# Block inverses in the recurrence: transposes on VectorE, predicated copies for masked subtractions, and a new order on ScalarE

## The chip, the cores and the metric

The kernel runs on one core of one Trainium2 chip, in one launch. The metric is the time of one execution on the device, in microseconds (us); several executions are run and the median is taken.

## The reference, cut to what matters

Two layers of a decoder trunk over 512 tokens of width 1024. Layer 0 mixes the tokens with two linear recurrences of 8 heads x 64 each, an RWKV-7 group and a gated DeltaNet group. Both need, for each chunk of 64 tokens and each head, the inverse of a unit lower triangular 64x64 matrix (below in the form of the second group; the first is a scan over tokens that the kernel also computes by chunks):

```python
a_mat = jnp.where(strict, jnp.einsum('bhnik,bhnjk->bhnij', k_beta, k) * decay, 0.0) + jnp.eye(C, dtype=f32)
tri = functools.partial(lax.linalg.triangular_solve, left_side=True, lower=True, unit_diagonal=True)
u = tri(a_mat, v * beta[..., None])
w = tri(a_mat, k_beta * jnp.exp(g)[..., None])
...
def step(S, inp):
    v_new = u_c - jnp.einsum('bhck,bhkv->bhcv', w_c, S)
    o_c = jnp.einsum('bhck,bhkv->bhcv', q_c * jnp.exp(g_c)[..., None], S) + jnp.einsum('bhij,bhjv->bhiv', qk_c, v_new)
    S = S * jnp.exp(g_last)[..., None] + jnp.einsum('bhck,bhcv->bhkv', k_c * jnp.exp(g_last - g_c)[..., None], v_new)
```

Around it stand large projections and MLPs, and in layer 1 two attention groups; the change doesn't touch them.

## The kernel before

The program has one instruction list per engine, written out by hand, and semaphores between them. Layer 0's input projection comes first, then the recurrence, then layer 0's output projection and MLP, then layer 1.

**The recurrence** is a loop over s = 0 to 4. For s < 4 it prepares block s of 128 tokens (two chunks of 64, one on partitions 0 to 63, the other on 64 to 127, for 8 heads side by side in 512 columns): it is "ahead". For s > 0 it runs the states of block m = s - 1 through its two chunks and makes that block's output: it is "behind". The two kinds of work are interleaved in each engine's list, and each engine keeps its order. So s = 0 has only the preparation, s = 1 to 3 have both, and s = 4 has only the work behind.

**The inverse.** R stands for the RWKV heads, G for the gated heads. `QI` holds the transposed inverse so far (it begins as the 2x2 blocks, masked by VectorE, with the identity added by GpSimd), `TI` the inverse itself, `LT` the full triangle. `first_inverse` transposes `QI` into `TI`. Then come five levels, in which blocks of 2, 4, 8, 16 and 32 rows are joined to blocks of twice the size. A level in `level_products` is: TensorE multiplies `LT` by `TI` for R and then G (banks 0 and 1); VectorE multiplies by the mask `MERGE[:, lev + 1]` into `XM` (L1644); TensorE multiplies `QI` by `XM`; VectorE subtracts the result from `TI` (L1647). `level_turn` has TensorE transpose `TI` for R and G, with matmuls against the identity into banks 2 and 3 (L664), and ScalarE copies them to `QI` (L1181), which only the second product of the next level reads. The last level takes the factors the other way round and changes `QI` directly, so that no transposition follows it.

**What stands between the levels.** Each product or transposition by `both_halves` (L602) or `transposed` (L664) is 16 matmul calls of 64x64, and each fp32 call shows as two instructions. TensorE puts the work behind between the levels: `state_sums` and `chunk_out` (L719, L602) after level 0, `turned_out` (L579), the transposition of the output rows, before level 4. VectorE puts `chunk_out` (L1682 to L1688) and the next block's `decay_steps` (L1598) between levels 1 and 2, `out_var` (L1692 to L1697) after level 2, `out_scaled` (L1701, L1702) and the next block's `scaled_rows` (L1603, L1604) between levels 3 and 4. ScalarE runs `out_squares` (L1185, L1187) after the turn of level 1, `out_rms` (L1191, L1193, each with a table load) and the next block's `decays` (L1135, L1137) after that of level 2, before that of level 3. GpSimd scales two tensors of the next block (L2008, L2009) as soon as the first of the `decays` is there. The next block's inputs (L629, L579) wait for the last level's result (`inv_done`).

## Time and profile before

| | |
|---|---|
| median of 3 runs | 1593.75 us (1593.73 to 1594.44) |
| the profiled execution | 1590.02 us |
| its span, from the first to the last instruction | 1588.2 us |
| TensorE busy in it | 1480.8 us (93%) |
| VectorE, ScalarE, GpSimd busy | 724.6 us (46%), 601.9 us (38%), 574.5 us (36%) |
| mean granted TensorE clock | 0.97 of full |
| the recurrence | from about 250 to 491 us of the span |

PE is TensorE, DVE VectorE, ACT ScalarE, POOL GpSimd. A busy share is a mean over stages with different limits; for the change the stretch of the recurrence is what has to be read. The profiled execution is one execution, not one of the three of the median.

### The profile page before, as it was taken

The page shows a single profiled execution, that of the slowest core. Times are in us where ns is not written, and L with a number is a line of the kernel's source. Part 1 is how long each engine was busy: PE and PEld are TensorE (multiplying, and loading weights), DVE is VectorE, ACT ScalarE, POOL GpSimd, SP SyncE. Part 2 cuts the span into 40 slices and gives each one's busy share as a digit, 9 for nine tenths or more (in the row PEclk, how much of TensorE's full clock was granted, in tenths as well). Part 3 has the DMA queues.
Part 4 walks back from the last instruction along what each step waited for, and adds up shares of the span by engine and source line. Part 5 has one row for each costly group of instructions (what it writes and reads, how often), then busy time and mean ns, then how long its engine had stood idle before and what let it go on. Part 6 is the DMA issues. An engine that isn't in the chain of part 4 may idle for free.

```text
span 1588.2 us, 27117 instructions
## 1 busy us (share of the span) xinstructions
PE 1480.8 (93%) x11601; PEld 1193.2 (75%) x11601; DVE 724.6 (46%) x1065; ACT 601.9 (38%) x866; POOL 574.5 (36%) x266
## 2 busy tenths in 40 slices
PE   5999888989987999999999799996989999999998
PEld 4787568888885788888888588773457888888886
DVE  4787775686655341313222602885843413223131
ACT  4424453243334431313232424547854413233231
POOL 4343331010002344343434323233954343443432
PEclk9999899999978999999999899997999999999999
DMA  4332100000011322323223312220002332323231
GB/s 127 89 93 80 53 27 3 4 3 4 4 55 60 100 90 96 105 81 105 87 98 97 89 54 87 73 80 0 1 28 80 106 97 89 106 79 106 79 106 53
DMA packets 128403, 110.18 MB, mean 69 GB/s; under 512 B 10678, under 2 KB 126512, under 8 KB 128304
## 3 DMA queue, kind: packets, MB, share of 16 engines
q1 hardware_dynamic: 126944, 107.06, 21.6%
q8 instruction: 80, 1.31, 0.4%
q10 hardware_dynamic: 1360, 1.65, 0.3%
q14 instruction: 19, 0.16, 0.0%
HBM read 106.60 MB, written 2.10 MB: 68 GB/s over the span
## 4 chain that ended last, share of the span: by engine, by line
PE 76%; DVE 12%; ACT 7%; issue 3%; POOL 1%; ACTq 1%; DVEq 0%; POOLq 0%
PE ps L476 20%; PE ps L481 20%; PE ps L477 20%; PE ps L602 5%; PE ps L664 2%; DVE lower L1864 2%; DVE lower L1860 1%; POOL lower L2066 1%; DVE upper L1467 1%; PE ps L617 1%; PE ps L610 1%; ACT lower L1368 1%; PE ps L579 1%; PE ps L719 1%; PE ps L822 0%
## 5 line engine op out<-in xcount | busy, mean ns | idle before, releaser
L2034 POOL TENSOR_TENSOR w_lo<-lower,w_hi 128x2048 fp32r<-128x2048 f32 x84 | 387.6, 4614 | 642.0 <-ACT w_hi L1024 642.0
L476 PE MATMUL ps<-h_hi,w_hi 128*128 128x512 f32 x792 | 316.0, 399 | 8.9 <-ACT h_hi L1029 5.9
L477 PE MATMUL ps<-h_hi,w_lo 128*128 128x512 f32 x792 | 314.7, 397 | 0.0
L1024 ACT ACTIVATE w_hi<-lower 128x2048 fp32r<-128x2048 f32 x84 | 160.2, 1907 | 242.8 <-PE ps L481 242.8
L481 PE MATMUL ps<-h_lo,w_hi 128*128 128x512 f32 x792 | 201.6, 395 | 0.4
L476 PE MATMUL ps<-a_hi,w_hi 128*128 128x512 f32 x480 | 189.1, 394 | 0.0
L477 PE MATMUL ps<-a_hi,w_lo 128*128 128x512 f32 x480 | 189.1, 394 | 0.0
L476 PEld LDWEIGHTS ps<-h_hi,w_hi 128*128 128x128 f32 x792 | 150.3, 190 | 46.4 <-issue 11.5
L477 PEld LDWEIGHTS ps<-h_hi,w_lo 128*128 128x128 f32 x792 | 150.4, 190 | 36.1 <-issue 0.5
L481 PEld LDWEIGHTS ps<-h_lo,w_hi 128*128 128x128 f32 x792 | 148.7, 188 | 37.4 <-DVE h_lo L1574 1.7
L1809 DVE TENSOR_TENSOR lower<-lower,ps 128x512 f32<-128x512 f32 x64 | 44.0, 688 | 268.7 <-PE ps L481 268.7
L1793 DVE SCALAR_TENSOR_TENSOR lower<-ps,lower 128x512 f32<-128x512 f32 x64 | 44.3, 692 | 226.0 <-PE ps L481 209.9
L2013 POOL TENSOR_TENSOR pw_lo<-lower,pw_hi 128x1024 fp32r<-128x1024 f32 (+1 forms) x31 | 79.0, 2550 | 127.0 <-ACT pw_hi L1036 127.0
L1255 ACT ACTIVATE lower<-lower 128x512 f32<-128x512 f32 x64 | 40.5, 633 | 215.9 <-DVE lower L1793 215.9
L481 PE MATMUL ps<-a_lo,w_hi 128*128 128x512 f32 x480 | 121.5, 395 | 0.0
L476 PE MATMUL ps<-x_hi,pw_hi 128*128 128x512 f32 (+1 forms) x248 | 101.4, 409 | 5.7 <-issue 4.3
L481 PEld LDWEIGHTS ps<-a_lo,w_hi 128*128 128x128 f32 x480 | 90.1, 188 | 21.7
L477 PEld LDWEIGHTS ps<-a_hi,w_lo 128*128 128x128 f32 x480 | 90.1, 188 | 21.4
L476 PEld LDWEIGHTS ps<-a_hi,w_hi 128*128 128x128 f32 x480 | 90.0, 188 | 21.1
L1798 DVE TENSOR_TENSOR h_lo<-lower,h_hi 128x512 fp32r<-128x512 f32 x64 | 97.3, 1521 | 6.9 <-ACT h_hi L1257 6.9
L477 PE MATMUL ps<-x_hi,pw_lo 128*128 128x512 f32 (+1 forms) x248 | 99.2, 400 | 0.0
L602 PE MATMUL ps<-lower 64*64 64x64 f32 x2112 | 69.7, 219 | 6.4 <-DVE upper L1632 3.0
(352 smaller groups left out, 2092.7 us busy)
## 6 DMA issues: line engine op xcount, KB each, us to landing
lower<-in_mlp_w_dram SPq DMA_DIRECT2D x64, 1024.0 KB, 5.2
lower<-in_ev_w_in_dram SPq DMA_DIRECT2D x30, 512.0 KB, 3.8
lower<-in_od_w_in_dram SPq DMA_DIRECT2D x10, 1024.0 KB, 5.2
lower<-in_ev_w_out_dram SPq DMA_DIRECT2D x4, 1024.0 KB, 5.2
lower<-in_od_w_out_dram SPq DMA_DIRECT2D x4, 1024.0 KB, 5.0
out_dram<-lower SPq DMA_DIRECT2D x4, 512.0 KB, 3.2
lower<-in_od_w_in_dram SPq DMA_DIRECT2D x6, 256.0 KB, 3.8
upper<-in_x_dram ACTq DMA_DIRECT2D x1, 1024.0 KB, 8.4
```

Of the source, the lines that this page charges most:

```text
L476: pe.matmul(o, wh, xh, start=(i_ == 0), stop=False)
L477: pe.matmul(o, wl, xh, start=False, stop=False)
L481: mm = pe.matmul(o, wh, xl, start=False, stop=(i_ == n_ - 1))
L602: mm = pe.matmul(ps[part, b, h_ * HD:(h_ + 1) * HD], mats[part, j, q, :], vals[part, j, q, :], start=(start and h_ == 0), stop=True, skip_ ...
L664: mm = pe.matmul(ps[part, b, h_ * HD:(h_ + 1) * HD], x[part, h_ // 2, h_ % 2, :], IDENT[part, part], start=True, stop=True)
L1024: act.activation(WH[:, u % 2, :, 0:w], RAW[:, u % 2, :, 0:w], ACT.Copy).then_inc(hi_ready, 1)
L1255: act.activation(sq, sq, ACT.Square).then_inc(h1_sq, 1)
L1793: dve.scalar_tensor_tensor(out=SQT[:, b % 4, :], in0=src(q)[:, :], scalar=0.0, in1=RS[2 * l + 1], op0=ALU.max, op1=mul).then_inc(bank_read, 1)
L1798: dve.tensor_tensor(HL[:, b, :], SQT[:, b % 4, :], as_f32(HH[:, b, :]), sub).then_inc(h1_ready, 1)
L1809: dve.tensor_tensor(XT[:, k, :], XT[:, k, :], src(q_m2[l] + k)[:, :], add)\
L2013: pool.tensor_tensor(PWL[:, u % 3, :, 0:w], PRAW[:, u % 2, :, 0:w], as_f32(PWH[:, u % 3, :, 0:w]), ALU.subtract).then_inc(pw_lo, 1)
L2034: pool.tensor_tensor(WL[:, u % 2, :, 0:w], RAW[:, u % 2, :, 0:w], as_f32(WH[:, u % 2, :, 0:w]), ALU.subtract)\
```

## The change

1. **Transposes.** TensorE's `first_inverse` and `level_turn` go, with ScalarE's and VectorE's copies behind them. VectorE transposes in 32x32 blocks from SBUF to SBUF: `QI` to `TI` at the start, `TI` to `QI` after levels 0 to 3. Up to then no block of the inverse is larger than 32x32, so that a blockwise transposition is the whole one.
2. **Joining.** The first product of a level is not masked: ScalarE copies it from PSUM with the factor -1. VectorE then writes the second product into `TI` (or, in the last level, `QI`) only where the mask is set, with `copy_predicated`. The last level's mask is built for the upper side.
3. **Order.** `level_products` is split into `below_blocks` and `joined_blocks`. ScalarE's copies of level 2 stand ahead of `out_squares`, those of level 3 ahead of `out_rms`, those of level 4 behind `out_rms` and `decays`. On TensorE the first products of level 4 stand ahead of `turned_out`, the second ones behind it. Two semaphores go, and with them TensorE's wait for `inv_q` at the start of a block.

```diff
@@ TensorE
             def turned_inputs(s):
                 pe.wait_ge(e_gtri, s + 1)
                 if s > 0:
-                    pe.wait_ge(inv_q, 2 * (LAST - 1) * s)
                     pe.wait_ge(inv_done, 2 * s)
...
-            def transposed(b, x, done):
-            def first_inverse(s):
-            def level_turn(s, lev):
-            def level_products(s, lev):
+            def below_blocks(s, lev):
                 n = 2 * LAST * s + 2 * lev
                 for g, (lt, ti) in enumerate(((LTR, TIR), (LTG, TIG))):
-                    pe.wait_ge(inv_t, n + g + 1)
+                    pe.wait_ge(inv_t, n + (2 if lev == 0 else g + 1))
                     both_halves(g, lt, ti, True).then_inc(inv_x, 1)
+
+            def joined_blocks(s, lev):
+                n = 2 * LAST * s + 2 * lev
                 for g, (qi, xm) in enumerate(((QIR, XMR), (QIG, XMG))):
                     pe.wait_ge(inv_xm, n + g + 1)
...
                 if ahead:
-                    level_turn(s, 0)
                     for lev in range(1, LAST - 1):
-                        level_products(s, lev)
-                        level_turn(s, lev)
+                        below_blocks(s, lev)
+                        joined_blocks(s, lev)
+                    below_blocks(s, LAST - 1)
                 if behind:
                     turned_out(m)
                 if ahead:
-                    level_products(s, LAST - 1)
+                    joined_blocks(s, LAST - 1)
@@ ScalarE
-            def first_inverse(s):
-            def level_turn(s, lev):
-                for g, qi in enumerate((QIR, QIG)):
-                    act.wait_ge(inv_turn, 2 * (LAST - 1) * s + 2 * lev + g + 1)
-                    act.activation(flat4(qi[s % 2]), bank[2 + g], ACT.Copy).then_inc(inv_q, 1)
+            def below_blocks(s, lev):
+                for g, xm in enumerate((XMR, XMG)):
+                    act.wait_ge(inv_x, 2 * LAST * s + 2 * lev + g + 1)
+                    act.activation(flat4(xm), bank[g], ACT.Copy, scale=-1.0).then_inc(inv_xm, 1)
...
                 if ahead:
-                    level_turn(s, 0)
-                    level_turn(s, 1)
+                    below_blocks(s, 0)
+                    below_blocks(s, 1)
                 else:
                     weight_hi(0)
+                if ahead:
+                    below_blocks(s, 2)
                 if behind:
                     out_squares(m)
                 if ahead:
-                    level_turn(s, 2)
+                    below_blocks(s, 3)
                 if behind:
                     out_rms(m)
                 if s < TT - 1:
                     decays(s + 1)
                 if ahead:
-                    level_turn(s, 3)
+                    below_blocks(s, 4)
@@ VectorE
+            def blocks(m):
+                return m.bitcast(I32).unsqueeze(1).unsqueeze(1).broadcast_to([P, PAIRS, 2, HD])
...
             def first_inverse(s):
-                dve.wait_ge(inv_t0, 2 * s + 1)
-                dve.wait_ge(inv_t, 2 * LAST * s + 1)
-                dve.tensor_copy(TIG, by_head(bank[1])).then_inc(inv_t, 1)
-
-            def level_products(s, lev):
+                for g, (ti, qi) in enumerate(((TIG, QIG), (TIR, QIR))):
+                    dve.wait_ge(inv_q0, 2 * s + g + 1)
+                    dve.transpose(flat4(ti), flat4(qi[s % 2])).then_inc(inv_t, 1)
+
+            def joined_blocks(s, lev):
                 n = 2 * LAST * s + 2 * lev
-                for g, xm in enumerate((XMR, XMG)):
-                    dve.wait_ge(inv_x, n + g + 1)
-                    dve.tensor_tensor(xm, by_head(bank[g]), mask(MERGE[:, lev + 1, :]), mul).then_inc(inv_xm, 1)
-                for g, x in enumerate((TIR, TIG) if lev < LAST - 1 else (QIR[s % 2], QIG[s % 2])):
+                inner = lev < LAST - 1
+                for g, x in enumerate((TIR, TIG) if inner else (QIR[s % 2], QIG[s % 2])):
                     dve.wait_ge(inv_y, n + g + 1)
-                    dve.tensor_tensor(x, x, by_head(bank[g]), sub)\
-                       .then_inc(inv_t if lev < LAST - 1 else inv_done, 1)
+                    dve.copy_predicated(x, blocks(MERGE[:, lev + 1, :]), by_head(bank[g]))\
+                       .then_inc(inv_t if inner else inv_done, 1)
+                if inner:
+                    for g, (ti, qi) in enumerate(((TIR, QIR), (TIG, QIG))):
+                        dve.wait_ge(inv_t, n + 2 + g + 1)
+                        dve.transpose(flat4(qi[s % 2]), flat4(ti)).then_inc(inv_q, 1)
```

## Rows read from the trace of the kernel before

**Rows 1.** The page's chain that ended last, by engine.

```profile
PE 76%; DVE 12%; ACT 7%; issue 3%; POOL 1%; ACTq 1%; DVEq 0%; POOLq 0%
```

**Rows 2.** Windows: us; busy us of PE, PEld, DVE, ACT, POOL; clock; DMA.

```profile
250.30:283.30 33.00, 30.03 (x993) 29.81 (x993) 18.15 (x27) 7.14 (x12) 5.79 (x7) 1.00 0.02 4
339.90:396.45 56.55, 50.98 (x1503) 48.75 (x1503) 40.29 (x66) 21.14 (x35) 6.42 (x5) 1.00 0.02 3
453.20:491.10 37.90, 22.67 (x360) 21.30 (x360) 18.52 (x30) 13.39 (x20) 4.52 (x1) 0.62 0.23 75
```

**Rows 3.** Groups by line: busy us, mean ns, then idle before and its releaser.

```profile
L664 PE MATMUL ps<-lower 64*64 64x64 f32 x1152 | 38.2, 219 | 0.0
...
L1181 ACT ACTIVATE lower<-ps 128x512 f32<-128x512 f32 x16 | 9.6, 597 | 35.1 <-PE ps L664 35.1
...
L1467 DVE SCALAR_TENSOR_TENSOR upper<-upper,lower 128x512 f32<-128x512 f32 x36 | 47.6, 1322 | 1.3
...
L1644 DVE TENSOR_TENSOR lower<-ps,lower 128x512 f32<-128x512 f32 x40 | 27.4, 690 | 33.1 <-PE ps L602 33.1
...
L1609 DVE TENSOR_SCALAR lower<-lower 128x512 f32<-128x512 f32 x4 | 1.7, 427 | 0.1
```

**Rows 4.** Timeline of the first block: start us, us, engine, line, operation.

```profile
255.41 2.08 PE L602 MATMUL ps<-lower 64*64 64x64 f32 x64 [0.69 <-ACT lower L1167]
...
259.29 2.08 PE L664 MATMUL ps<-lower 64*64 64x64 f32 x64
...
278.44 2.03 PE L602 MATMUL ps<-lower 64*64 64x64 f32 x64
...
260.48 0.60 ACT L1181 ACTIVATE upper<-ps 128x512 f32<-128x512 f32 x1 [5.13 <-PE ps L664]
...
252.24 1.27 POOL L2025 TENSOR_TENSOR upper<-upper,lower 128x512 f32<-128x512 f32 x1 [1.24 <-DVE upper L1633]
```

**Rows 5.** Timelines by engine of the third block (s = 2), and the last block's end.

```profile
367.98 1.86 PE L664 MATMUL ps<-lower 64*64 64x64 f32 x58
...
379.26 2.08 PE L602 MATMUL ps<-lower,upper 64*64 64x64 f32 x64 [1.65 <-DVE lower L1644]
...
373.86 0.69 DVE L1647 TENSOR_TENSOR lower<-lower,ps 128x512 f32<-128x512 f32 x1 [0.25 <-PE ps L602]
...
378.52 1.28 DVE L1644 TENSOR_TENSOR lower<-ps,lower 128x512 f32<-128x512 f32 x2
...
382.00 0.68 DVE L1692 TENSOR_REDUCE lower<-lower 128x8 f32<-128x512 f32 x1
...
383.38 0.16 DVE L1697 TENSOR_SCALAR lower<-lower 128x8 f32<-128x8 f32 x1
...
387.74 1.58 DVE L1701 TENSOR_TENSOR lower<-lower 128x512 f32<-128x512 f32 x1
...
383.94 1.28 ACT L1191 ACT_TABLE_LOAD   x1
...
388.14 0.60 ACT L1181 ACTIVATE upper<-ps 128x512 f32<-128x512 f32 x1
...
387.59 1.18 POOL L2008 TENSOR_TENSOR upper<-upper 128x512 f32<-128x512 f32 x1 [31.46 <-ACT upper L1135]
...
450.01 0.69 DVE L1647 TENSOR_TENSOR lower<-lower,ps 128x512 f32<-128x512 f32 x1 [0.25 <-PE ps L602]
```

**Rows 6.** Windows on TensorE: us, busy (instructions), granted clock (1.00 is full).

```profile
319.30:322.60 3.30, 1.73 (x60) 1.00 0.04 7
450.90:453.40 2.50, 0.03 (x1) 1.00 0.61 167
...
455.70:476.20 20.50, 16.85 (x275) 0.50 0.13 41
987.80:990.80 3.00, 0.00 (x0) 1.00 0.00 0
991.60:995.00 3.40, 3.40 (x11) 0.50 0.92 301
```

More of the change, by code:

```diff
@@ L659, in key_values @@
                 both_halves(2, MK, VR[s % 2], True).then_inc(f_mkv, 1)
[L661 to L673 removed]
+            def below_blocks(s, lev):
                 n = 2 * LAST * s + 2 * lev
                 for g, (lt, ti) in enumerate(((LTR, TIR), (LTG, TIG))):
[L677 removed]
+                    pe.wait_ge(inv_t, n + (2 if lev == 0 else g + 1))
                     both_halves(g, lt, ti, True).then_inc(inv_x, 1)
+            def joined_blocks(s, lev):
+                n = 2 * LAST * s + 2 * lev
                 for g, (qi, xm) in enumerate(((QIR, XMR), (QIG, XMG))):
                     pe.wait_ge(inv_xm, n + g + 1)
[L681 removed]
+                    if lev == 0:
+                        pe.wait_ge(inv_q0, 2 * s + 2)
+                    else:
                         pe.wait_ge(inv_q, 2 * (LAST - 1) * s + 2 * (lev - 1) + g + 1)
@@ L759, in _ @@
                     state_reads(m, 1)
-                if ahead:
-                    first_inverse(s)
                 if behind:
@@ L1974, in _ @@
                 b = 1 << lev
[L1975 removed]
+                last = int(lev == LEVELS - 1)
+                low = FULL[:, lev, :].rearrange("p (n q w) -> p n q w", q=2, w=b)[:, :, last, :]
                 t.link(pool.memset(low, 1.0))
[L1978 to L1979 removed]
+                select(low, 0 if last else -b, [[-2 * b, P // (2 * b)], [0, b]], 1, 0.0)
+                select(low, b - 1 if last else 2 * b - 1, [[2 * b, P // (2 * b)], [0, b]], -1, 0.0)
             for g in range(16):
```

37 lines of the change are left out of this document (11 added, 26 removed).

## The prediction

> **What bounds the kernel now.** I read the chain of waits first: matmuls own three quarters of it [rows 1], and the recurrence is the only long stretch of short matmuls. Then the windows by block: the first block of 128 tokens takes 33.0 us, the third 56.55, the tail behind the last block 37.9; TensorE is busy for 30.0 and 51.0 us of the two blocks, at full clock [rows 2]. So TensorE leads in the blocks and leaves some 5 us to waits. The groups by line then give the price of each operation [rows 3], and two timelines show the order: the first block, where nothing else is interleaved [rows 4], and the third, which stands for the second as well [rows 5].
>
> **What goes and what comes.** Per block ten TensorE transposes of 16 calls go; a call shows as two instructions, so 320 per block, 1280 in all, of which [rows 3] has the 1152 of one form. A pair of them, one for each kind of head (64 instructions), is a third of a level of 5.76 us in the first block (worked out below), 1.92 us. Five pairs are 9.6 us per block. Also gone are ScalarE's nine copies behind them (0.60 us each) and VectorE's ten mask multiplications and one copy. In come ten negating ScalarE copies, ten predicated copies in place of ten subtractions, and ten VectorE transposes. VectorE runs 20 operations per block where it ran 21. No DMA is issued or moved; GpSimd builds as many masks, long before. TensorE's wait for the copied transposes at the head of a block also goes: nothing, since the wait beside it, for the inverse, ends later.
>
> **Prices that the trace lacks.** The predicated copy reads PSUM and SBUF like L1644, 0.69 us [rows 3]; the transpose reads and writes 512 fp32 of SBUF. For both the nearest cheap row is the one-source L1609 at 0.43, the dear one the three-operand L1467 at 1.32. I take 0.69 for both, because both stream 512 elements once, as L1644 does. The Trainium skill, Vector Engine (DVE) Microarchitecture Reference, section on the reshape front-end, says the 32x32 array sustains one element per cycle per lane; by that the transpose would also be near 0.7, an estimate no row here tests.
>
> **First block.** A product of one kind of head takes 0.96 us: four products and a pair of transposes of the same length fill a level, and from 255.41 to 278.44 four levels take 23.03 us, 5.76 each, so a sixth of that [rows 4]. A reader starts 1.19 us after its product starts (259.29 to 260.48). After the change a level is: product 0 to 0.96, the other kind's to 1.92; the ScalarE copy of the first 1.19 to 1.79; so the second product starts at 1.92 (TensorE is the later); its predicated copy 3.11 to 3.80; the next level at 3.86, against 3.84 of pure TensorE work. VectorE needs 4 x 0.69 = 2.8 of the 3.86, and its transposes are wanted 1.9 us into the next level: hidden, up to about 1.2 us each. Saved: 4 x (5.76 - 3.86) = 7.6. The start: GpSimd hands over the last input at 253.51 (252.24 + 1.27), a transpose of 0.69 makes 254.3 where 255.41 stood: 1.1. The last level (278.44 to the block's end at 283.30 [rows 2]) stays, but the row scaling of the next block now stands close ahead of its predicated copies: 0.3 lost. Sum **8.4**.
>
> **Third block.** Its first transposes stand in front of a solve that also waits for VectorE and ScalarE, so of their 1.9 us I count only 0.1 up to where the older tokens' sums end and the level's transposes begin, at 367.8 before (58 of their 64 instructions from 367.98) [rows 5], 367.7 now. From there, new order:
> - level 1's first products 367.7 to 369.6, second 369.6 to 371.5; predicated copies 370.8 to 372.4; both transposes to 373.8.
> - VectorE's output sums and decay step: they ran from 374.46 (373.86 + 0.60) to 378.52, 4.1 us; now 373.8 to 377.9. Level 2's products are done by 375.4, so TensorE **waits 3.3 us** where it waited 1.65 (row at 379.26).
> - Level 2's predicated copies 377.9 to 379.2, level 3's first products from 378.7, transposes to 380.6, variances (382.00 to 383.54, 1.55) to 382.15. Level 3's second products 380.6 to 382.5, level 4's first 382.9 to 384.8.
> - Here the moved order bites. ScalarE's root with its two table loads and the next block's decays ran 383.94 to 388.14, 4.2 us, ahead of a copy that was ready about then. Now they start at 382.2 and end at 386.4, and level 4's copies, ready at 384.1, stand behind them: they end at 387.6. TensorE, behind, has only the output turns.
> - The two output scalings: 0.69 each without company, 1.58 at 387.74 with GpSimd's scaling (387.59) beside it. GpSimd starts on the decays' first half, 385.9, so I leave the first at 0.69 and give the second 1.5: 387.5. By the Trainium skill, SBUF — State Buffer, section Who interferes with whom, one of the two holds a shared port for its whole instruction; if GpSimd held it for both of its operations, the scaling would end some 1.2 us later, and so would the block.
> - Turn to 388.3; last second products 388.3 to 390.2; predicated copies to 391.1 (390.44 + 0.69); next block at 391.3. It was 396.45 [rows 2]: **5.2** saved, the second block the same.
>
> **Last block.** No decays and no GpSimd company, a decay step of 0.6 less: the root ends at 384.6 in the frame above, copies at 385.8, scalings and turns at 386.7, last products from 386.7, last predicated copy ends 389.5. Before, this block ended at 450.70 (450.01 + 0.69), 54.25 after its start at 396.45, in the frame 394.1: **4.6**. The tail has none of this change; it only moves.
>
> With the clock full: 8.4 + 5.2 + 5.2 + 4.6 = **23.4**.
>
> **The clock.** This is what I expect to take part of it back. After TensorE idled 2.5 us (450.9) and 3.0 us (987.8) the granted clock stood at half, 1.2 GHz, soon after; after the 1.65 us inside 319.3 to 322.6 it stayed at 2.4 [rows 6]. The new wait of 3.3 us is of the first sort, and so may be the 3.4 us around the output turns, which hold 1.2 us of work. A half-clock stretch of 3.4 us, the shortest here, costs up to 1.7 where TensorE leads. Behind the first wait the products of level 3 delay the root by about 1.5; behind the second the last product and the next block's inputs lose 2 to 3. I count four such stretches in three blocks, 1.6 each: 6.4. The first block has no such gap.
>
> **Sum.** 23.4 - 6.4 = 17.0. The profiled execution took 1590.02 us, 1.8 beyond its span, so it would become 1573; but the median of the runs is 1593.75, 3.7 above it, and I set the forecast by that: **1577 us**.
>
> **Rivals.**
> - *Full clock throughout*: the waits fall apart into short ones. For it: the clock held through all blocks now [rows 2]. Against: [rows 6]. 1570.
> - *VectorE becomes the bound*: one of the new operations takes 1.32. If the predicated copy: a level 4.5, first block 5.2 saved; in the others 1.0 at level 1, 1.3 at level 2, 0.9 at the end are lost, leaving 2.0, 2.0, 1.4; sum 10.6, less 3 for the clock, 1586. If the transpose: 7.6 + 2.6 + 2.6 + 2.0 = 14.8, less 3, 1582. Both: nothing is left, 1594. For it: the two operations have no row, and VectorE runs nearly unbroken from 370.8 to 384.8. At the cheap end, 0.43, at most 3 us more are gained, since ScalarE's table loads then end last: 1574.
> - *It does not do what it says*: TensorE's 9.6 us per block only turn into waits, and the two table loads take what is left; each block then gains 2 and the first 5: 1583 to 1587. Against: 5.76 against 3.86 in the first block is plain arithmetic.
> - *Slower*: the clock falls at the 3.3 us wait and stays down. In the tail it stood at 0.50 for 20.5 us though TensorE was busy for 16.85 of them, 82% [rows 6]; a changed block is busy for 41.3 of 51.3 us, 80%. Half clock doubles TensorE's part, so each microsecond of it on the path costs up to 0.5; 5.2 us are eaten by some 10.4 us of it per block, 23.4 by 47 in all. If the three blocks are down for 60 us, 1600. Against: work at half clock fills the gaps that keep it down, and other falls lasted 3.4 us.
>
> **Chances.** Forecast with some half-clock stretches 0.50 (its own range 1573 to 1581); full clock 0.17; one VectorE price dear 0.15; little done 0.05; both dear 0.05; slower by the clock 0.08. The range goes from below the full-clock case to the edge of the dear predicated copy: 1569 to 1588, 8 in 10. What a measurement here can tell from no change is 0.2%, 3.2 us: faster beyond it 0.85, within it 0.07, slower 0.08.
>
> **What would show it.** First block: no L664, levels every 3.9 us, block 24.6 us instead of 33.0. DVE rows of 0.69 for predicated copy and transpose. Third block near 51 us plus its half-clock part; a TensorE wait of about 3 us ahead of level 3; ScalarE's level-4 copy right behind the second exponential. PEclk below 1.00 in blocks 2 to 4. It is wrong if the new VectorE rows lie above 1.1, or if the clock stays at 0.50 for more than 10 us of a block.

## The result, and the profile after

The changed kernel took **1568.49 us** (median of 4 runs, 1568.3 to 1569.15); the kernel before took 1593.79 beside it (4 runs, 1593.73 to 1594.44). The ratio is 0.9841, with a 95% interval of 0.9824 to 0.9858: faster, by 25.3 us. The forecast was 1577 and the range 1569 to 1588; the sign was right, the forecast gain was 8.5 us too small, and the result lies 0.5 us below the range. One execution of the kernel before, of the 19 that ran beside the first experiments, took 4278.79 us; it counts as slow and is left out of every figure here. The profiled execution took 1568.51 us, its span is 1566.4 us, 21.8 us shorter than that of before.

The chain that ended last, by engine, of the kernel after, answers to [rows 1]: TensorE's part fell by two points.

```profile
PE 74%; DVE 13%; ACT 7%; issue 3%; POOL 2%; ACTq 1%; DVEq 0%; POOLq 0%
```

Windows of the kernel after, with the columns of [rows 2]: the first block's end (the start is shifted by the 2.0 us that the recurrence begins later), the second, third and last block, TensorE's wait inside the third and the stretch that follows it, and the tail.

```profile
252.33:278.40 26.07, 23.12 (x673) 22.67 (x673) 16.92 (x26) 7.73 (x13) 5.78 (x7) 0.87 0.02 4
278.40:328.31 49.91, 41.82 (x1183) 39.32 (x1183) 37.20 (x62) 21.32 (x36) 6.43 (x5) 1.00 0.01 3
328.31:379.58 51.27, 43.17 (x1183) 40.67 (x1183) 38.91 (x65) 21.32 (x36) 6.42 (x5) 0.97 0.01 3
379.58:429.43 49.85, 44.21 (x1214) 41.75 (x1214) 35.27 (x62) 20.26 (x34) 2.64 (x2) 0.97 0.02 4
363.60:366.00 2.40, 0.02 (x2) 0.00 (x0) 2.33 (x6) 1.26 (x2) 0.00 (x0) 1.00 0.00 0
366.08:369.50 3.42, 3.05 (x57) 3.05 (x58) 3.39 (x8) 0.60 (x1) 0.00 (x0) 0.50 0.02 5
431.92:468.75 36.83, 20.12 (x360) 18.80 (x361) 16.57 (x29) 13.42 (x20) 4.56 (x1) 0.67 0.22 75
```

TensorE ran 1183 instructions in a block instead of 1503, the 320 fewer of the forecast. The second block kept the full clock and took 49.91 us instead of 56.6; the third took 51.27, and what sets it apart is a mean clock of 0.97: one stretch of 3.42 us at half clock, right behind a wait of TensorE. The last block has such a stretch too (0.97), and the first one of 6.8 us (0.87). The pieces add up to the difference of the two spans: first block 6.9 us shorter (44.21 to 37.28 from the recurrence's start), second 6.7, third 5.3, last 4.6, tail 0.9; the work ahead of the recurrence took 2.0 longer and that behind it 0.7, none of which the change touches. Sum 21.7, of the 21.8 measured.

Groups by line of the kernel after, columns as in [rows 3]: the predicated copies, ScalarE's negating copies and VectorE's transposes.

```profile
L1634 DVE COPY_PREDICATED lower<-lower,ps 128x512 f32<-128x512 int32 x36 | 25.9, 731 | 33.9 <-PE ps L602 33.5
L1163 ACT ACTIVATE lower<-ps 128x512 f32<-128x512 f32 x40 | 23.5, 595 | 50.7 <-PE ps L602 50.6
L1639 DVE STREAM_TRANSPOSE lower<-lower 128x512 f32<-128x512 f32 x16 | 10.3, 685 | 0.0
```

Both unknown prices were 0.69 in the forecast; measured, the predicated copy takes 0.73 and the transpose 0.69.

Timeline of the first block after, answering to [rows 4], on TensorE: the first products of each level, then the next block's first matmuls.

```profile
256.33 3.68 PE L602 MATMUL ps<-lower 64*64 64x64 f32 x64 [0.63 <-DVE lower L1627]
...
261.96 2.08 PE L602 MATMUL ps<-lower 64*64 64x64 f32 x64
...
265.81 2.08 PE L602 MATMUL ps<-lower 64*64 64x64 f32 x64
...
273.54 2.08 PE L602 MATMUL ps<-lower 64*64 64x64 f32 x64
...
278.40 1.10 PE L628 MATMUL ps<-upper,lower 128*128 128x512 f32 x2 [0.92 <-DVE upper L1634]
```

A level takes 3.85 us (261.96 to 265.81), where the forecast had 3.86. The first one is longer, 5.63 us (256.33 to 261.96): its first products take 3.68 us instead of 2.08, at half clock, and its second ones are slowed a little too.

Timelines of the second block after, which ran at full clock, to be laid beside [rows 5]: VectorE, ScalarE, GpSimd and TensorE, in that order.

```profile
310.54 1.29 DVE L1639 STREAM_TRANSPOSE lower<-lower 128x512 f32<-128x512 f32 x2
311.75 0.65 DVE L1673 TENSOR_TENSOR lower<-lower 128x512 f32<-128x512 f32 x1
...
315.77 1.33 DVE L1634 COPY_PREDICATED lower<-lower,ps 128x512 f32<-128x512 int32 x2
317.00 1.29 DVE L1639 STREAM_TRANSPOSE lower<-lower 128x512 f32<-128x512 f32 x2
318.21 0.65 DVE L1683 TENSOR_REDUCE lower<-lower 128x8 f32<-128x512 f32 x1
...
319.56 0.16 DVE L1688 TENSOR_SCALAR lower<-lower 128x8 f32<-128x8 f32 x1
...
322.97 1.69 DVE L1693 TENSOR_TENSOR upper<-upper,lower 128x512 f32<-128x512 f32 x1
...
318.67 0.60 ACT L1163 ACTIVATE lower<-ps 128x512 f32<-128x512 f32 x1 [0.34 <-PE ps L602]
319.29 1.28 ACT L1173 ACT_TABLE_LOAD   x1
...
323.43 1.06 ACT L1163 ACTIVATE lower<-ps 128x512 f32<-128x512 f32 x2
...
322.93 1.18 POOL L2000 TENSOR_TENSOR upper<-upper 128x512 f32<-128x512 f32 x1 [28.28 <-ACT upper L1121]
...
316.55 5.95 PE L602 MATMUL ps<-lower 64*64 64x64 f32 x192 [2.83 <-DVE lower L1634]
```

Three things are to be seen. The wait ahead of level 3 is there, 2.83 us where 3.3 was forecast, and it is for VectorE's predicated copies, which stand behind the output sums. Many of VectorE's linked instructions start closer together than their durations: two transposes of 0.69 show as one row of 1.29, and the next instruction starts 1.21 after the first. And ScalarE's table load starts at 319.29, right behind its copies (318.67 + 0.60), though the variances, which begin at 318.21, are not done until 319.72 (319.56 + 0.16).

### The profile page after: what moved, and what is told of

Read it like the earlier page. It is cut to its first block, busy times and chain, and to the rows that moved or that the text cites. A ratio compares the mean times of both kernels' runs of the same rounds, so it can differ in the third digit from the quotient of the medians.

```text
span 1566.4 us, 24561 instructions
## 1 busy us (share of the span) xinstructions
PE 1450.3 (93%) x10321; PEld 1159.1 (74%) x10321; DVE 719.4 (46%) x1061; ACT 603.0 (38%) x870; POOL 574.1 (37%) x266
## 3 DMA queue, kind: packets, MB, share of 16 engines
q10 hardware_dynamic: 1360, 1.65, 0.3%
## 4 chain that ended last, share of the span: by engine, by line
PE 74%; DVE 13%; ACT 7%; issue 3%; POOL 2%; ACTq 1%; DVEq 0%; POOLq 0%
PE ps L476 21%; PE ps L477 21%; PE ps L481 21%; PE ps L602 5%; POOL lower L2058 2%; DVE lower L1855 2%; DVE lower L1851 1%; DVE upper L1450 1%; PE ps L617 1%; ACT lower L1351 1%; PE ps L610 1%; PE ps L706 1%; PE ps L579 1%; DVE lower L1840 1%; DVE lower L1634 1%
## 5 line engine op out<-in xcount | busy, mean ns | idle before, releaser
L481 PEld LDWEIGHTS ps<-a_lo,w_hi 128*128 128x128 f32 x480 | 90.1, 188 | 21.7
L602 PE MATMUL ps<-lower 64*64 64x64 f32 x2112 | 73.3, 227 | 11.6 <-DVE lower L1634 7.9
```

The source lines that it names most:

```text
L481: mm = pe.matmul(o, wh, xl, start=False, stop=(i_ == n_ - 1))
L602: mm = pe.matmul(ps[part, b, h_ * HD:(h_ + 1) * HD], mats[part, j, q, :], vals[part, j, q, :], start=(start and h_ == 0), stop=True, skip_ ...
```

## Experiments

### How far one kernel's executions lie apart

The kernel before was run again unchanged, and so was the kernel after; three more kernels moved everything behind the recurrence's start by a little, with 5 or 10 linked one-element copies on VectorE:

```diff
             scaled_rows(0)
+            for _ in range(5):
+                t.link(dve.tensor_copy(VAR[:, 0:1], PC[:, 0:1]))
             gated_inputs()
```

The kernel before again, with no edit:

> The kernel before, unchanged, with a new profile. Its profiled execution took 1590.02 us where its timed ones took 1593.75; the kernel after showed no such gap (1568.51 against 1568.49). Theory A: where the half-clock stretches fall differs between executions, so the new profile again differs from the runs by up to 4 us, and the granted clock of the timed executions (as the results list it) lies below 0.970. Theory B: the offset belongs to profiling this kernel and comes again as 3.7 us with the same clock in all.

The kernel before with five copies:

> The kernel before with five small dependent VectorE copies (0.15 us each, some 0.8 us in all) ahead of the recurrence, on the path. Theory A (the clock's falls hang on when TensorE idles): the time moves by something other than +0.8, between -3 and +4 us. Theory B (timing does not hang on it): +0.8 us.

The kernel after with five, and with ten:

> The kernel after with the same 0.8 us ahead of the recurrence. Theory A: between -3 and +4 us against 1568.5, and half-clock stretches at other places of blocks two to four, of 3.4 us each, costing about 1.4 where they meet products. Theory B: 1569.3.

> The kernel after with ten such copies, 1.6 us. Theory A: between -2 and +5 us against 1568.5; Theory B: 1570.1. If my forecast's four half-clock stretches in three blocks were the usual case and the two of the profiled execution luck, one of the two delayed kernels shows three or four and blocks two to four some 3 us longer.

The kernel after again, with no edit:

> The changed kernel once more, with nothing edited, for the spread of its own executions. Theory A: what differs between executions of one kernel is where the half-clock stretches fall outside the second and third block; so its median lies between 1567 and 1573 us (the first one 1568.5; the copies with a few small linked VectorE instructions more 1571.7 and 1572.1), its second and third block are again 49.9 us at full clock or 51.2 with one half-clock stretch of 3.4 us, and the rest of the span differs with its microseconds at half clock. Rival: 1568.5 was a lucky placing, and the usual time is 1575 or more, with two stretches in each block.

| kernel | median, us | runs, us | ratio to before (95%) |
|---|---|---|---|
| before again | 1591.43 | 10: 1588.12 to 1595.94 | 0.9995 (0.9978 to 1.0013) |
| before, 5 copies | 1593.83 | 1591.42 to 1595.52 | 1.0003 (0.9990 to 1.0015) |
| after, 5 copies | 1572.09 | 4: 1570.47 to 1572.34 | 0.9863 (0.9834 to 0.9893) |
| after, 10 copies | 1571.65 | 1570.9 to 1571.99 | 0.9865 (0.9836 to 0.9893) |
| after again | 1569.46 | 5: 1567.2 to 1574.91 | 0.9858 (0.9837 to 0.9880) |

The kernel before, run again, spreads over 8 us. Its profiled execution lies 4 us above its own median, where the first one lay 3.7 below, so the offset does not belong to profiling. The small copies in the kernel before took it 1 us above the 1592.76 of the kernel before beside it, which their own 0.8 explains as well as the clock does. The profile of the repeated kernel before has a span of 1593.7 against 1588.2, yet its second and third block are the same to 0.01 us. These are its windows; the second of them is the third block.

```profile
286.73:343.31 56.58, 51.01 (x1503) 48.78 (x1503) 38.65 (x63) 21.12 (x35) 6.42 (x5) 1.00 0.02 4
343.31:399.88 56.57, 51.00 (x1502) 48.77 (x1503) 40.30 (x66) 21.13 (x35) 6.43 (x5) 1.00 0.01 3
```

The 5.5 us lie in the other stretches, where the granted clock was at half, 1.2 GHz, for 108 us in all against 95. The profile of before with five copies agrees: a span of 1592.0 us, 105 of them at half clock. So the profiled execution of before, on which the forecast's pieces rest, was near the fast end of its kernel, and a difference of two spans is uncertain by some 5 us, while single blocks are not. After again and with five copies, the same block shows itself with no, one and two half-clock stretches. First after again (second and third block), then after with five copies (second and third), then after with ten (second and third):

```profile
280.48:331.94 51.46, 43.36 (x1183) 40.84 (x1183) 37.34 (x62) 21.33 (x36) 6.42 (x5) 0.97 0.01 3
331.94:381.84 49.90, 41.82 (x1183) 39.31 (x1183) 38.82 (x65) 21.33 (x36) 6.42 (x5) 1.00 0.01 3
```

```profile
278.68:331.48 52.80, 44.69 (x1183) 42.21 (x1183) 37.31 (x62) 21.33 (x36) 6.43 (x5) 0.94 0.01 3
331.48:382.74 51.26, 43.16 (x1183) 40.66 (x1183) 38.92 (x65) 21.33 (x36) 6.42 (x5) 0.97 0.01 3
```

```profile
279.48:330.64 51.16, 43.05 (x1183) 40.57 (x1183) 37.28 (x62) 21.32 (x36) 6.41 (x5) 0.97 0.01 3
330.64:381.81 51.17, 43.07 (x1183) 40.58 (x1183) 38.90 (x65) 21.32 (x36) 6.42 (x5) 0.97 0.01 3
```

49.9, 51.2 to 51.5 and 52.8: a stretch of 3.4 us costs 1.3 to 1.6 us, near the 1.6 of the forecast. The last block took 49.7 us in all four profiles, each time with one stretch. So the second to fourth block together hold two stretches in the profile of after, two in after again, four with five copies and three with ten. The forecast counted four. It was at the upper end of what this kernel does, not outside it; the expectation for the kernel with ten copies had named three or four stretches, in one of the two, as the sign that the two of the first profile were luck, and both kernels show it.

The places repeat. In nine of the twelve blocks a stretch begins 37.5 to 39.4 us into the block, right behind the wait ahead of level 3, which lasts 2.83 us in the second and third block and 2.23 in the last. One more begins 47.0 us into a block, behind the output turns (after again), and one 18.9 us into it, among the products of the state (five copies). In the three profiles of the kernel before, where that wait is 1.65 us or shorter, none of the nine blocks has a stretch.

The two kernels with copies took some 3 us more than after. Two stretches more and the 0.8 us of the copies account for it with five; with ten it is one stretch and 1.6 us.

### Each half of the change without the other

In both kernels of this section TensorE's list has the order of the change, with level 4's first products ahead of the output turns, so what they gain includes what that order gives them, and no run has the order alone on the kernel before. The first is the kernel before with the transposes on VectorE, but with VectorE's mask multiplication and subtraction as before and no copy by ScalarE:

```diff
-                dve.wait_ge(inv_t0, 2 * s + 1)
-                dve.tensor_copy(TIG, by_head(bank[1])).then_inc(inv_t, 1)
+                for g, (ti, qi) in enumerate(((TIG, QIG), (TIR, QIR))):
+                    dve.transpose(flat4(ti), flat4(qi[s % 2])).then_inc(inv_t, 1)
...
+                if inner:
+                    for g, (ti, qi) in enumerate(((TIR, QIR), (TIG, QIG))):
+                        dve.transpose(flat4(qi[s % 2]), flat4(ti)).then_inc(inv_q, 1)
```

> Half of the change alone: VectorE transposes in place of TensorE's, but the products are masked and subtracted by VectorE as before (four 0.69 us operations and two transposes per level, no ScalarE copy of the first product). TensorE's 9.6 us per block go. Theory A (TensorE's work is what is saved): the first block saves a little less, since VectorE's six operations of 0.69 make 4.1 us per level against 3.84; blocks two to four save 3 to 4; total 1572 to 1576. Rival (the path over VectorE decides): a level gets 5 us, total 1580 to 1586.

Measured: 1591.36 us (10 runs, 1589.2 to 1594.28), ratio 0.9991 (0.9978 to 1.0003): nothing, which neither theory had; even the rival, that the path over VectorE decides, expected 1586 at most. TensorE's rows of its first block, then its long wait in the second, then VectorE's rows ahead of that wait:

```profile
262.70 2.08 PE L602 MATMUL ps<-lower,upper 64*64 64x64 f32 x64 [0.64 <-DVE lower L1625]
...
267.96 2.08 PE L602 MATMUL ps<-lower,upper 64*64 64x64 f32 x64 [1.25 <-DVE lower L1625]
...
320.92 4.32 PE L602 MATMUL ps<-lower 64*64 64x64 f32 x76 [4.70 <-DVE lower L1625]
```

```profile
314.94 1.30 DVE L1633 STREAM_TRANSPOSE lower<-lower 128x512 f32<-128x512 f32 x2
316.16 0.65 DVE L1667 TENSOR_TENSOR lower<-lower 128x512 f32<-128x512 f32 x1
...
320.18 1.28 DVE L1625 TENSOR_TENSOR lower<-ps,lower 128x512 f32<-128x512 f32 x2
```

With six operations per level VectorE is the bound: in the first block a level takes 4.7 to 5.3 us. In the second the mask multiplication of level 2 (L1625, 320.18) stands behind the output sums, and TensorE waits 4.70 us for it. Its clock then stood at half for 6.8 us of each of the two blocks. What TensorE no longer did it waited for.

The other half, again with TensorE's new order and also with ScalarE's: TensorE's turns of `TI` and ScalarE's copies of them stay, and the negating copies and predicated copies come (with them the transposes of the first inverse on VectorE).

```diff
-                    dve.tensor_tensor(x, x, by_head(bank[g]), sub)\
+                    dve.copy_predicated(x, blocks(MERGE[:, lev + 1, :]), by_head(bank[g]))\
...
+            def below_blocks(s, lev):
+                for g, xm in enumerate((XMR, XMG)):
+                    act.activation(flat4(xm), bank[g], ACT.Copy, scale=-1.0).then_inc(inv_xm, 1)
```

> The other half alone: TensorE's transposes of the levels and ScalarE's copies of them stay, the first inverse's two transposes are VectorE's, and the joining is by negating ScalarE copies and predicated copies. Theory A: TensorE's 1.92 us per level stay, so the first block stays at levels of 5.76 us and saves 1 us at its start; VectorE has less to do (two operations per level instead of four), which lets the output sums start earlier: about 1 us per block; total 1587 to 1591. Rival (VectorE's relief is the larger part of the gain): 1578 to 1583.

Measured: 1585.16 us (1583.9 to 1585.81), ratio 0.9948 (0.9930 to 0.9967), between the two theories. Its third block took 52.59 us at full clock, 4.0 below before, with TensorE busy for 48.90 of them:

```profile
338.08:390.67 52.59, 48.90 (x1439) 46.78 (x1439) 34.62 (x57) 25.67 (x44) 6.43 (x5) 1.00 0.02 4
```

So the halves give 0.9991 and 0.9948, together 0.9841 to 0.9858, some 24 us where the sum would be 10, although the order is counted in both. The rows fit this reading: each of the two relieves an engine behind which the other one stands. In the first kernel TensorE waits for VectorE, in the second it is busy for 48.90 of 52.59 us. How much of the second one's 8 us is the order's, and how much the joining's, stays open.

### TensorE's turns put back without a use

To price the turns alone, the kernel after was given them back, eight a block, into two unused banks that nobody reads:

```diff
+            def unused_turn(s, lev):
+                for g, ti in enumerate((TIR, TIG)):
+                    pe.wait_ge(inv_t, 2 * LAST * s + 2 * (lev + 1) + g + 1)
+                    for h_ in range(NH):
+                        for part in HALVES:
+                            pe.matmul(ps[part, 2 + g, h_ * HD:(h_ + 1) * HD], ti[part, h_ // 2, h_ % 2, :],
+                                      IDENT[part, part], start=True, stop=True)
```

> The kernel after plus TensorE's eight level transposes per block, into banks 2 and 3, which nobody reads: 7.7 us of TensorE work per block come back, and nothing waits for its result. Theory A (TensorE's own time is the path): first block +7.6, blocks two to four +3 to +5 each (they also fill waits and keep the clock up), total 1585 to 1591. Rival (the chain product, copy, product, copy is the path): under +8 in all, 1576 or less.

Measured: 1588.31 us (7 runs, 1587.61 to 1589.77), ratio 0.9972 (0.9960 to 0.9985). The first block grew by 7.6 us: four pairs of 1.9, all of it on the path, as the forecast's 4 x (5.76 - 3.86) says. The second and third took 55.1 each with one half-clock stretch, 3.9 more than a block of after with one stretch, since a part of the turns fell into the waits for VectorE. The total lies in the range of theory A, that TensorE's own time is the path. So the turns are worth about 19 of the 24 us once the rest of the change is there.

### The order on TensorE undone

The first products of level 4 behind the turn of the output rows, as before the change:

```diff
-                    below_blocks(s, LAST - 1)
                 if behind:
                     turned_out(m)
                 if ahead:
+                    below_blocks(s, LAST - 1)
                     joined_blocks(s, LAST - 1)
```

> The kernel after, with level 4's first products behind the transposition of the output rows on TensorE, as before. The output rows are ready (second scaling's end) about 2.2 us after level 4's first products end; moved behind, the products, their copy and the second products come after: +1.9 to +2.5 us in blocks two to four each, total 1574 to 1576. Rival (the last scaling and the half clock hide it): within 2 us, 1568 to 1570.

Measured: 1579.05 us (1577.35 to 1581.07), ratio 0.9913 (0.9893 to 0.9932), 10.6 above the 1568.5 of after. TensorE's rows of the second block:

```profile
321.69 0.66 PE L579 MATMUL ps<-lower 128*128 128x128 f32 x4 [2.61 <-DVE lower L1692]
323.30 0.73 PE L579 MATMUL ps<-lower,upper 128*128 128x128 f32 x4 [0.96 <-DVE upper L1693]
323.95 5.39 PE L602 MATMUL ps<-lower 64*64 64x64 f32 x128
```

It waits 2.61 us for VectorE's output scaling where after waits 0.61, with the level's first products still to do, and the clock fell to half behind it. The two copies of the first products now lie between the turns and the last products, too. The second, third and last block took 53.3, 54.7 and 51.6 us with one, two and one stretches. Against blocks of the changed kernel with the same number of stretches (51.3 to 51.5, 52.8, 49.7) that is some 1.9 us more each, the low end of what was expected. It makes 5.6 us, and two stretches more than in after make another 2.8: nearly all of the 8.9 by which the span is longer. So the undoing cost more than the 5.5 to 7.5 us expected because it brought half-clock stretches with it, and a count of those differs between executions too.

### New order on all engines

The last level's products ahead of the output turns on TensorE, its copies ahead of the next block's decays on ScalarE, its predicated copies ahead of the next block's row scaling on VectorE:

```diff
@@ TensorE
-                if behind:
-                    turned_out(m)
                 if ahead:
                     joined_blocks(s, LAST - 1)
+                if behind:
+                    turned_out(m)
@@ ScalarE
-                if s < TT - 1:
-                    decays(s + 1)
                 if ahead:
                     below_blocks(s, 4)
+                if s < TT - 1:
+                    decays(s + 1)
@@ VectorE
-                if s < TT - 1:
-                    scaled_rows(s + 1)
                 if ahead:
                     joined_blocks(s, 4)
+                if s < TT - 1:
+                    scaled_rows(s + 1)
```

> The changed kernel, with TensorE's second products of level 4 ahead of the output turns, ScalarE's copies of level 4 between the root and the next block's decays, and VectorE's predicated copies of level 4 ahead of the next block's row scaling. Theory A (decays, row scaling beside GpSimd and the turns stand on the path of the last level): second and third block fall from 49.9 (full clock) or 51.2 (one half-clock stretch) to about 47.5 to 49, the last block by 1, the total by 4 to 6 us against the changed kernel: 1563 to 1567. Rival: the row scaling and decays, now later, hold up the next block's first products by as much: within 1 us of the changed kernel, 1568 to 1572.

And the same with VectorE's decay step of the next block behind level 2:

```diff
-                if s < TT - 1:
-                    decay_steps(s + 1)
                 if ahead:
                     joined_blocks(s, 2)
+                if s < TT - 1:
+                    decay_steps(s + 1)
```

> As the kernel with the new order of level 4, and VectorE's decay step of the next block behind the predicated copies of level 2 instead of ahead of them. Theory A: TensorE's wait ahead of level 3, 2.8 us in the changed kernel, is made of VectorE's output sums and this step; 0.6 us less of it per block in the second and third, 1.2 us in all beyond the kernel with the level-4 order alone, 1562 to 1566. Rival: the decay step only moves to ahead of the variances and makes level 4 and the root later: no difference to that kernel.

Measured: 1569.08 us (1567.6 to 1569.47), ratio 0.9853 (0.9836 to 0.9870), and 1567.46 (1566.57 to 1568.04), ratio 0.9839 (0.9825 to 0.9854); after again, beside them, 1569.46. The windows of the first of them, second and third block:

```profile
277.01:324.51 47.50, 41.53 (x1183) 39.33 (x1183) 35.97 (x62) 19.72 (x32) 6.92 (x8) 1.00 0.01 3
324.51:375.99 51.48, 44.45 (x1183) 42.03 (x1183) 37.48 (x65) 21.66 (x37) 5.96 (x6) 0.93 0.01 3
```

The second block fell to 47.5 (46.9 in the other kernel), by 2.4 and 3.0 us, as expected. The third did not gain: 51.5, with two half-clock stretches. The totals lie 2.1 and 1.5 us above what theory A expected of them; that of the first is where its rival had it, within 1 us of the changed kernel, and after again's own runs spread over 7.7 us, so no gain in the total is shown.

### TensorE's wait filled

Into the wait ahead of level 3, 96 unused instructions (2.8 us) that write an unused bank:

```diff
+            def unused_products(n):
+                for _ in range(n):
+                    for h_ in range(NH):
+                        for part in HALVES:
+                            pe.matmul(ps[part, 2, h_ * HD:(h_ + 1) * HD], LTR[part, h_ // 2, h_ % 2, :],
+                                      IDENT[part, part], start=True, stop=True)
...
                         joined_blocks(s, lev)
+                        if lev == 2 and behind:
+                            pe.wait_ge(r_mkv, s + 1)
+                            unused_products(3)
```

> The changed kernel with 96 unused TensorE instructions (three times 16 calls of 64x64 into an unused bank, about 2.8 us at full clock) behind the level-2 products in the second to fourth block, where TensorE waits 2.8 us for VectorE. Nothing of the result depends on them. Theory A: this wait is what the half-clock stretch of these blocks follows on; with it filled, second and third block run at full clock throughout, 49.9 to 50.3 us each, and the last block is some 1 us shorter: total 1565 to 1569. Rival 1: the stretch follows on the later wait around the output turns; then it stays where it was and the total is that of the changed kernel, 1568 to 1572. Rival 2: the wait was covering less than 2.8 us and the filler itself is in the way: each block 0.5 to 1 us longer, 1570 to 1575.

Measured: 1566.72 us (5 runs, 1566.46 to 1567.9), ratio 0.9838 (0.9824 to 0.9853), against 0.9858 (0.9837 to 0.9880) for after again in the same comparison. The totals' intervals overlap; the blocks show more. Second and third block, and the place of the former wait:

```profile
276.28:326.25 49.97, 44.65 (x1278) 42.16 (x1279) 37.24 (x62) 21.32 (x36) 6.42 (x5) 1.00 0.02 3
326.25:376.15 49.90, 44.61 (x1278) 42.10 (x1279) 38.80 (x65) 21.32 (x36) 6.41 (x5) 1.00 0.01 3
362.50:366.50 4.00, 3.96 (x136) 3.83 (x133) 4.00 (x7) 1.23 (x2) 0.00 (x0) 1.00 0.02 4
```

Both blocks kept the full clock, and 96 instructions more cost nothing. The last block had one half-clock stretch all the same, 18.3 us into it, earlier than any that followed on this wait. The profiles of the other kernels sort themselves by this wait. Where TensorE hardly idles ahead of level 3 (this kernel, the one with the unused turns and the one with the joining alone), none of the nine blocks has a stretch there, and five have one 18.0 to 18.9 us into the block. Where it idles for 4.1 to 4.7 us (the transposes alone), all three have one there. So the falls behind this wait hang on it, and there is a second place, among the products of the state. All these kernels wait there for 0.88 us, 15.5 us into the block, where TensorE's first transposes stood before; that this brings the falls is not shown.

Then the filler together with the whole new order, with 96 and with 64 instructions (`unused_products(2)`):

> The new order of level 4 and the later decay step together with the 96 unused TensorE instructions (2.8 us) behind the level-2 products. The wait there is 2.2 us in this order, so the filler overlaps it by 0.6. Theory A (a stretch at half clock costs some 2 us of a block here, and two of them hid what the order saves): second and third block both near 47.5 us (46.9 and the 0.6), without half clock, total 1560 to 1563. Rival (the order saves only in one of the blocks): third block at 50 us or more even at full clock, total 1564 to 1567.

> The same with 64 unused instructions (1.9 us) in the wait of 2.2 us. Theory A: the filler is then wholly hidden; second and third block 46.9 us each if the clock holds, total 1559 to 1562, some 1 us below the kernel with 96. Rival: a shorter filler lets the clock fall again in one or both blocks, each 1.5 to 4.5 us longer, 1562 to 1567.

Measured: 1565.54 (1563.2 to 1568.07), ratio 0.9834 (0.9820 to 0.9849), and 1565.13 (1563.61 to 1567.97), ratio 0.9835 (0.9821 to 0.9849). The theory that promised 47 us in both blocks fell: the third took 50.1 in both kernels. The totals lie in the ranges of the two rivals, but not for their reasons as written: the third block was not at full clock with the longer filler, and the shorter filler kept the clock no worse. Windows of the kernel with 64: second block, third block, and the half-clock stretch in the third; below, VectorE's rows at the third block's start.

```profile
280.47:327.38 46.91, 43.25 (x1247) 41.13 (x1247) 35.83 (x62) 19.82 (x32) 6.49 (x8) 1.00 0.02 4
327.38:377.45 50.07, 44.93 (x1247) 42.56 (x1247) 37.66 (x65) 21.76 (x37) 5.98 (x6) 0.97 0.01 3
347.92:351.33 3.41, 3.41 (x72) 3.41 (x68) 0.53 (x2) 1.74 (x3) 0.00 (x0) 0.50 0.00 0
```

```profile
327.13 1.57 DVE L1596 TENSOR_TENSOR lower<-lower,upper 128x512 f32<-128x512 f32 x1
328.62 0.68 DVE L1597 TENSOR_TENSOR lower<-lower,upper 128x512 f32<-128x512 f32 x1
329.22 0.68 DVE L1709 TENSOR_TENSOR lower<-lower,upper 128x512 f32<-128x512 f32 x1
...
330.54 0.69 DVE L1712 TENSOR_TENSOR upper<-upper 128x512 f32<-128x512 f32 x1
331.14 0.68 DVE L1601 TENSOR_TENSOR lower<-ps,lower 128x512 f32<-128x512 f32 x1
```

In this order the row scaling and the three operations of the finished output (L1709, L1710, L1712) stand between the block's end and its successor's first VectorE work. The second block is spared the three, since no older block's output goes ahead of it: in the third, L1601 starts 3.76 us after the block's start, in the second 1.86. Of these 1.9 us 1.7 are left at the last masks of the preparation, and the half-clock stretch has the other 1.5 of the 3.2 between the two blocks. So the order gains 3.0 us in one block and, worked out from this, about 1.3 in the other.

These kernels are the fastest ones, 1565.1 to 1565.5. Against the 1568.5 and 1569.5 of the kernel after that is 0.2 to 0.3%, and the intervals of the ratios overlap: the direction is shown by the blocks' windows, the total barely.

## Why the prediction was right or wrong

The mechanism was the forecast one: TensorE's transposes went, the rest of each block moved up, a wait ahead of level 3 came, and half-clock stretches followed on it. The steps that failed are two sizes in the sum: the 5.2 us saved by the second and third block each, which measured 6.7 in the second, at full clock (5.3 in the third, with a half-clock stretch), and the 6.4 us that the clock was to take back, which measured 2.8 in the profiled execution. The miss of the range itself is slight: 1568.49 lies 0.5 us below it, and the same kernel's 1569.46, run again, lies inside.

**The prices were right.** Predicated copy 0.73, transpose 0.69, both taken as 0.69. The rival of a dear VectorE falls. The Trainium skill, Vector Engine (DVE) Microarchitecture Reference, section on the reshape front-end, has the transpose pass one element per cycle and lane; the trace agrees, since the transpose takes as long as VectorE's other operations that pass 512 elements once (0.69).

**First block: right but for the clock.** 8.4 was forecast. A level takes 3.85 us, the start gained 1.1, the last level stayed at 4.86 (273.54 to 278.40) without the 0.3 that I took off. 6.9 came out because the first level took 5.63 us, 1.8 more than the others, at half clock. "The first block has no such gap" was wrong as a promise. All four profiles of the changed kernel, those with copies included, have a stretch there, of 3.4 or 6.8 us, and of the three of the kernel before only the repeated one has, of 3.4. In after (from 253.4) and after again it begins before the place where TensorE's list differs; in the two with copies it begins in the idle time that TensorE's transposes used to fill. Whether the change makes or lengthens it is open.

**Second and third block: the mis-sized term.** "5.2 saved" at full clock; 6.7 were. In us from the block's start, forecast against measured in the second block: output sums begin at 33.9 against 33.35, level 3's first products at 38.8 against 38.15, the root's table load at 42.3 against 40.9, next block at 51.4 against 49.9. Two reasons account for it. Some 0.7 went by level 3: level 1's predicated copies began 0.3 earlier than I had them, and I had strung the linked copies and transposes at their shown 0.69 where each linked pair takes 1.21 to 1.23 to the next start. The same stringing cost another 0.3 by the end of the variances. The last 0.4 is the table load: I started it when the variances are done (319.72), but it started at 319.29, as soon as ScalarE was free. Together that is 1.4 to 1.5 us a block, 2.9 of the total.

**The clock: the mis-sized count.** "I count four such stretches in three blocks, 1.6 each: 6.4." The price holds, 1.3 to 1.6. After's profile has two in the three blocks, some 2.8 us, and that is 3.6 us, the largest part of the miss. Part of it is luck of the executions, since the four profiles have two, two, four and three. The wait ahead of level 3 does bring them, in nine of twelve blocks; at the output turns, my second place, one of twelve has one. There I had TensorE without a product for 3.5 us but for the turns; it was 2.8 (322.50 to 325.30). The rival of a full clock throughout, at 1570, was nearest in number, and it was wrong as well: the clock did fall, while the blocks were shorter than it had them.

**Last block.** 4.6 forecast, 4.6 measured, but the agreement is luck: the measured block has one half-clock stretch in it that the 4.6 didn't hold. At full clock it would have been some 1.4 more, an estimate from the price of a stretch in the other blocks, for which I have no closer account than the same two reasons. The tail, said only to move, was 0.9 shorter.

**GpSimd beside VectorE.** I priced one scaling at 1.5 and the other at 0.69. The first took 0.68 without company, the second took 1.69 beside GpSimd's L2000, and the next block's L1586 1.67. The scaling ended at 324.66, 0.55 us after GpSimd's first operation (322.93 + 1.18), though its second followed at once. The next block's L1586 ended 0.55 us after GpSimd's second operation (326.25 against 325.70) in the same way. That fits the rule of the Trainium skill (SBUF — State Buffer, Who interferes with whom) that the shared port is held for a whole instruction, one at a time, and rules out the case of 1.2 us later.

**The sum.** Blocks and clock together were to give 17.0; they gave 23.5 (6.9, 6.7, 5.3, 4.6). The 6.5 between them: 2.9 by VectorE's chain and the table load in the second and third block, 3.6 by fewer half-clock stretches, 1.4 in the last block, less 1.5 in the first (6.4; the rest is rounding). Added to the median as the base, which the later runs of before (medians 1591.4 to 1593.8) bear out, that is 1570.2, and with the tail's 0.9 1569.3, within 1 us of the result.

**It does little, or slower.** Both fall. But the kernel with the transposes alone shows the first of them nearly word for word: TensorE's time turned into waits. The other half is what kept it from happening. Against the slower case I wrote that "other falls lasted 3.4 us"; that was read too narrowly, since in the profile of before four of twelve half-clock stretches last 3.4 us, and seven 6.8 to 20.5. In the second to fourth block of the changed kernel none outlasted 3.4.

**Open:** why one execution has a half-clock stretch behind the same wait and another does not, and why some fall 18 to 19 us into a block. The runs show where they fall, not what decides. Also open is what the order alone would do to the kernel before.

## What to carry to other kernels

When work moves off the leading engine, list the next one's operations in order and check that its chain is shorter than what remains; here the same move was worth nothing without the cut in VectorE's list and some 19 us with it. String linked VectorE instructions at their distance from start to start in a timeline, not at their mean duration, and start a table load when its engine is free, not when its data are. Count half-clock stretches from several profiles: four of this kernel had two, two, four and three in the same three blocks, and two of the kernel before differ by 5 us. Compare single blocks instead of totals.

## What the runs showed of the hardware that was not expected

- Executions of one kernel spread over 8 us of 1592, and two profiles of it differ by 5.5 us in span with 13 us more at half clock: 0.4 us for each.
- A wait of TensorE of 2.83 us (2.23 in the last block) was followed by 3.4 us at half clock in nine of twelve blocks of the changed kernel, at 1.3 to 1.6 us each; one of 1.65 us in none of six of the kernel before. Filling the 2.83 us with work that nobody reads kept 1.00 in both blocks and cost no time.
- Linked VectorE operations of 512 fp32 take 0.65 to 0.73 us each and start, depending on the pair, 0.56 to 0.73 apart, two thirds of them 0.59 to 0.63.
- A ScalarE table load of 1.28 us started 0.02 us behind the copy ahead of it and 0.43 before VectorE had finished the data of the activation that needs it.
- Two VectorE transposes of 128x512 fp32 in 32x32 blocks cost 1.21 us, where TensorE's pair of 32 calls cost 1.92 and two copies by ScalarE behind it.
